# GpSimd takes over the softmax denominators, their reciprocals and v's step in a hybrid decoder layer

## The chip, the cores and the metric

The kernel runs on one core of a Trainium2 chip. The metric is the device time of one execution in microseconds. Three runs of the kernel before took 1414.54 to 1418.3 us, median 1416.7; one further execution was profiled. All times below are microseconds (us) unless marked ns.

## The reference

One layer over 4096 tokens of width 1024. x is normalised by its root mean square and projected by one matrix into nine column groups: pool input and gate (256 each), three conv groups (256 each), q (512), k and v (128 each) and the attention gate (512). Cut to the part that the change touches:

```python
def sliding_window_attention(q, k, v, sinks):      # 8 query heads of 64, 2 key/value heads, blocks of 128
    kb = concatenate([k of the block before, k of this block])
    vb = concatenate([v of the block before, v of this block])
    scores = einsum('bnqkgd,bnskd->bnkgqs', qb, kb)
    scores = where(valid, scores + alibi, -1e30)   # a query sees the 128 keys up to itself
    p = softmax(concatenate([scores, sink], -1), -1)[..., :-1]
    return einsum('bnkgqs,bnskd->bnqkgd', p, vb)
```

The result is multiplied by silu of its gate, joined with the pool and conv branches, multiplied by w_out and added to x, and the sum is normalised.

## The kernel before, in words

The work has three stages. **Attention** walks over the 4096 tokens in 8 blocks of 512 (`NB`), each of 4 subtiles of 128. The **mixer** makes the conv and pool branches, and the **output** stage multiplies by w_out, by a scheme that needs sums and differences of w_out's quarters; these 28 sums (`Combos`) are made during attention, five per block in blocks 1 to 5 and the rest in block 6, and parked in HBM. Every matrix product is made in three matmuls, from a high and a low part of each operand. Each engine has its own queue, written out by hand in order, and waits on semaphores that others raise.

A block of the attention stage, engine by engine:

- **TensorE** (`body`, L1332): the first attend of the block before (L1238, two subtiles of probabilities times v), four q projections (the last holds `fold_sums`, L271, the sums of squares of the next x), the second attend, the v projection, then scores of subtile 0, gate projection 0, scores 1, gate 1, scores 2, gate 2, scores 3, gate 3, and k of the next block. Scores of a subtile (L1293) wait until VectorE has taken those before, since they share one PSUM region (`wide`). v's four transposes (`turn_v`) stand inside scores 1. In the last block v stands behind scores 0. The second attend waits for the mean of the next x's squares (`rstd_steps`), and each attend for GpSimd's mask.
- **VectorE** (`body`, L1113): the low part of k, the output of the first attend times the gate (L1220), the transposition of the last subtile's probabilities (L1073), low parts of q (L1093), the sums of w_out (L488 add, L500 low part), half of the next x's squares (L248), the mean (L282), then for each half of the heads `take_scores` (L1031: fold both key tiles into one, add the bias, row maximum), its negation (L1053) and the sinks' difference (L1054), `invert` (L1061: denominator L1065, reciprocal L1068), the transposition of the probabilities one subtile later, v's step (L1155, the difference of neighbouring blocks of v), the gates (L1103) and the eight pieces of the next x's low part (L339).
- **ScalarE** (`body`, L912): high parts of k and q, high parts of the sums (L496), the other half of the squares (L239), the scaling of x (L294), v out of PSUM before and after its transposes (L885, L977), exps (L903; with the sinks' exp, L900), the gates' tanh (L910), the high parts of the next x (L333).
- **GpSimd** (`body`, L856): the masks of the two last subtiles of the block before (L854), the root for the next x (L288), and per subtile the eight scalings of probabilities (L844). The masks of subtiles 0 and 1 stand behind subtile 2's.
- **SP** (`sync`, L711) issues transfers in order: the next x's first half (ScalarE issues the other), probabilities to HBM and back (`store_probs`, `load_probs`, which rearrange them), the sums' stores, xT's two halves (L728), y. In the last block it loads the mixer's first three weight chunks, CB, CA and GP (1 MB each, half of it from ScalarE's queue), ahead of the last probabilities of block 6.

A mask tile multiplies the probabilities of half the keys; v's step is subtracted the other way round for the upper 64 partitions.

Of the kernel before, what the change touches and what calls it, by code (L numbers as in the profile page):

```python
# [569 lines left out]
def attention_programs(nc, ctx, w, combos, banks, region, xs, spare, x_first, x_first_loaded, xT, xT_stored, xT_scratch, y, y_stored, x, ln_g,  # L570
# [53 lines left out]
    inv = sb("inv", [P, 2, HEADS])  # L624

# [85 lines left out]
    def sync(sp):  # L711
# [54 lines left out]
        for c in (CHUNK_CB, CHUNK_CA, CHUNK_GP):  # L766
# [3 lines left out]
        load_probs(sp, NB - 2, 3)  # L770
        sp.wait_ge(xT_stored[PIECES - 1], 16)
# [16 lines left out]
    def gpsimd(pool):  # L788
# [31 lines left out]
        def make_seen():  # L820
# [3 lines left out]
            nc.gpsimd.memset(masks[:, 2 * P:3 * P], 1.0).then_inc(bias_step, 1)  # L824
            pool.wait_ge(bias_step, 10)
# [30 lines left out]
        def body(n):  # L856
# [18 lines left out]
    def scalar(act):  # L875
# [20 lines left out]
        def exps(n, j, kv):  # L896
# [3 lines left out]
            nc.scalar.activation(sinkexp[:, b, heads], sinkdiff[:, b, heads], ACT.Exp)  # L900
            for t in range(GROUP):
                h = kv * GROUP + t
                last = nc.scalar.activation(probs[b][:, h], probs[b][:, h], ACT.Exp,  # L903
                                            bias=negmax[:, b, h:h + 1], accum_out=rowsum[:, b, h:h + 1])
            last.then_inc(exp_done, 1)
# [6 lines left out]
        def body(n):  # L912
# [21 lines left out]
            if final:  # L934
                act.wait_ge(st.lo_done, KT * NB)
                for c in (CHUNK_CB, CHUNK_CA, CHUNK_GP):
                    w.load(act, c, (2, 3))
            q_hi(n, 0)
            for s in combos.of_block(n, (0,)):
                combos.split_hi(act, s)  # L940
            if first:
                w.split_hi(act, CHUNK_Q + 1)
            if not first and not final:
                act.wait_ge(free(slot("g3")), earlier(n - 1, slot("g3")) + 1)
                st.square(act, n + 1)
            q_hi(n, 1)
            for s in combos.of_block(n, (1,)):
                combos.split_hi(act, s)
            if first:
                w.split_hi(act, CHUNK_G)  # L950
                st.square(act, 1)
            q_hi(n, 2)
            for s in combos.of_block(n, (2,)):
                combos.split_hi(act, s)
# [5 lines left out]
            if not final:  # L960
                for part in (0, 1):
                    st.scale(act, n + 1, part)
            for s in combos.of_block(n, (3, 4)):
                combos.split_hi(act, s)
# [14 lines left out]
            if not final:  # L979
                take_v()  # L980
# [12 lines left out]
                exps(n, 2, 1)  # L993
                for kk in range(st.AHEAD):
# [3 lines left out]
                for kv in range(KV):  # L998
                    exps(n, 3, kv)
            else:  # L1000
                for kv in range(KV):
                    exps(n, 0, kv)
                take_v()
                for kv in range(KV):
                    exps(n, 1, kv)
                gate_tanh(n, 0)
                exps(n, 2, 0)
                spread_v()
                exps(n, 2, 1)
                gate_tanh(n, 1)  # L1010
                w.split_hi(act, CHUNK_GP)
                for kv in range(KV):
                    exps(n, 3, kv)
                for t in (2, 3):
# [5 lines left out]
    def vector(dve):  # L1020
# [10 lines left out]
        def take_scores(n, j, kv):  # L1031
# [15 lines left out]
            for h in range(kv * GROUP, (kv + 1) * GROUP):  # L1047
# [5 lines left out]
            nc.vector.tensor_scalar(negmax[:, b, heads], rowmax[:, b, heads], -1.0, None, ALU.mult)  # L1053
            nc.vector.tensor_tensor(sinkdiff[:, b, heads], sinks[:, heads], rowmax[:, b, heads],  # L1054
                                    ALU.subtract).then_inc(max_ready, 1)
# [4 lines left out]

        def invert(m, b, kv):  # L1061

            heads = slice(kv * GROUP, (kv + 1) * GROUP)
            dve.wait_ge(exp_done, 2 * m + kv + 1)
            nc.vector.tensor_tensor(denom[:, b, heads], rowsum[:, b, heads], sinkexp[:, b, heads],  # L1065
                                    ALU.add).then_inc(den_step, 1)
            dve.wait_ge(den_step, 4 * m + 2 * kv + 1)
            nc.vector.reciprocal(inv[:, b, heads], denom[:, b, heads]).then_inc(den_step, 1)  # L1068
# [44 lines left out]
        def body(n):  # L1113
# [8 lines left out]
            if not first:  # L1122
                output(dve, n - 1, 0)
                turn_squares_of_probs(SUB * n - 1)
            make_q_lo(n, 0)
            make_combos(n, (0,))
            if not first and not final:
                st.square_more(dve, n + 1)
            for t in range(1, GROUP):
                if first:  # L1130
# [4 lines left out]
                if t == 3 and not final:  # L1135
                    st.mean(dve, n + 1)
# [1366 lines left out]
```

## Time and profile before

| | |
|---|---|
| median of 3 runs | 1416.7 us (1414.54 to 1418.3) |
| the profiled execution | 1414.61 us, its span 1412.7 us |
| mean granted clock of TensorE | 0.991 |
| busy: TensorE, VectorE, ScalarE, GpSimd | 96%, 83%, 39%, 25% of the span |
| attention stage | from the start to about 634 us |

The profile is of one execution. An engine's busy time is the union of its instructions; idle time is put down to what released the engine. The granted clock is TensorE's, as a share of 2.4 GHz. A matmul's end is modelled, and matmuls overlap, so the busy share of TensorE doesn't tell its rate.

### The profile page before, as it was taken

The page shows a single profiled execution, that of the slowest core. Times are in us where ns is not written, and L with a number is a line of the kernel's source. Part 1 is how long each engine was busy: PE and PEld are TensorE (multiplying, and loading weights), DVE is VectorE, ACT ScalarE, POOL GpSimd, SP SyncE. Part 2 cuts the span into 40 slices and gives each one's busy share as a digit, 9 for nine tenths or more (in the row PEclk, how much of TensorE's full clock was granted, in tenths as well). Part 3 has the DMA queues.
Part 4 walks back from the last instruction along what each step waited for, and adds up shares of the span by engine and source line. Part 5 has one row for each costly group of instructions (what it writes and reads, how often), then busy time and mean ns, then how long its engine had stood idle before and what let it go on. Part 6 is the DMA issues. An engine that isn't in the chain of part 4 may idle for free.

```text
span 1412.7 us, 20609 instructions
## 1 busy us (share of the span) xinstructions
PE 1354.7 (96%) x7070; PEld 1114.6 (79%) x7070; DVE 1173.6 (83%) x2381; ACT 550.8 (39%) x1421; POOL 358.4 (25%) x543
## 2 busy tenths in 40 slices
PE   6998999999999999889999999999999999999998
PEld 5776877777778787768888888888888788888886
DVE  5786869596978776649899998988999998898886
ACT  5654646565646564412122112121132243333332
POOL 5131313232322231220101011010110355455552
PEclk9999999999999999999999999999999999999999
DMA  9658393958585756875213033031327575554531
GB/s 214 204 141 307 99 312 120 289 166 274 173 238 209 195 204 167 295 164 199 97 52 134 29 137 134 15 134 45 148 96 266 236 244 173 179 179 155 170 106 75
DMA packets 117547, 239.18 MB, mean 169 GB/s; under 512 B 17488, under 2 KB 75216, under 8 KB 109776
## 3 DMA queue, kind: packets, MB, share of 16 engines
q1 hardware_dynamic: 93312, 214.24, 45.6%
q10 hardware_dynamic: 24144, 23.80, 6.9%
q8 instruction: 49, 0.80, 0.2%
q14 instruction: 42, 0.34, 0.1%
HBM read 139.44 MB, written 98.57 MB: 168 GB/s over the span
## 4 chain that ended last, share of the span: by engine, by line
PE 60%; DVE 19%; DMA 10%; ACT 4%; issue 3%; SPq 2%; POOL 1%; POOLq 0%; DVEq 0%; ACTq 0%
PE wide L346 12%; PE wide L347 12%; PE wide L348 12%; DMA xs<-in_x_dram 4%; DVE a_rows L1048 3%; DVE xT L339 3%; DVE m_tail L2047 3%; PE pair L1271 2%; PE pair L1272 2%; PE pair L1277 2%; PE turn L346 2%; PE pair L346 2%; PE pair L348 2%; PE turn L348 2%; PE pair L347 2%
## 5 line engine op out<-in xcount | busy, mean ns | idle before, releaser
L2047 DVE SCALAR_TENSOR_TENSOR m_tail<-m_tail,m_taps 128x512 f32<-128x512 f32 x480 | 338.3, 749 | 4.6
L844 POOL TENSOR_SCALAR a_rows<-a_rows,a_inv 128x128 f32<-128x128 f32 x256 | 91.8, 378 | 266.1 <-DVE a_inv L1068 203.9
L1271 PE MATMUL pair<-xT,w_hi 128*128 128x512 f32 x384 | 151.8, 395 | 3.6 <-DVE w_lo L410 3.6
L1272 PE MATMUL pair<-xT,w_lo 128*128 128x512 f32 x384 | 150.6, 392 | 0.0
L1277 PE MATMUL pair<-xT,w_hi 128*128 128x512 f32 x384 | 148.6, 393 | 0.0
L1789 POOL TENSOR_TENSOR operand_sums<-m_y 128x512 f32<-128x512 f32 x75 | 101.9, 1359 | 167.8 <-PE wide L348 116.7
L346 PE MATMUL wide<-x_first,w_hi 128*128 128x512 f32 x320 | 125.4, 392 | 0.0
L346 PE MATMUL wide<-xT,w_hi 128*128 128x512 f32 x320 | 125.2, 391 | 0.0
L348 PE MATMUL wide<-x_first,w_hi 128*128 128x512 f32 x320 | 124.6, 389 | 0.0
L348 PE MATMUL wide<-xT,w_hi 128*128 128x512 f32 x320 | 124.6, 389 | 0.0
L347 PE MATMUL wide<-x_first,w_lo 128*128 128x512 f32 x320 | 124.5, 389 | 0.0
L347 PE MATMUL wide<-xT,w_lo 128*128 128x512 f32 x320 | 124.5, 389 | 0.0
L108 POOL TENSOR_TENSOR pool_carrier<-pool_carrier 128x1 f32<-128x1 f32 x23 | 14.1, 615 | 394.0 <-DVE m_meanvar L2056 394.0
L1876 ACT ACTIVATE x_first<-operand_sums 128x512 fp32r<-128x512 f32 x80 | 50.4, 632 | 153.8 <-POOL operand_sums L1789 152.5
L1271 PE MATMUL wide<-xT,w_hi 128*128 128x512 f32 x256 | 101.3, 396 | 0.0
L1272 PE MATMUL wide<-xT,w_lo 128*128 128x512 f32 x256 | 99.7, 390 | 0.0
L1277 PE MATMUL wide<-xT,w_hi 128*128 128x512 f32 x256 | 99.7, 390 | 0.0
L903 ACT ACTIVATE a_rows<-a_rows,a_negmax 128x128 f32<-128x128 f32 x256 | 98.7, 387 | 0.0
L1271 PEld LDWEIGHTS pair<-xT,w_hi 128*128 128x128 f32 x384 | 72.8, 190 | 18.9 <-DVE w_lo L410 4.0
L1277 PEld LDWEIGHTS pair<-xT,w_hi 128*128 128x128 f32 x384 | 72.5, 189 | 18.1 <-DVE xT L339 2.9
L1272 PEld LDWEIGHTS pair<-xT,w_lo 128*128 128x128 f32 x384 | 72.7, 189 | 13.7
L1048 DVE CUSTOM_DVE_ANT_0 a_rows<-wide,a_bias,a_sinks 128x128 f32<-128x128 f32 x256 | 74.6, 348 | 2.3
(264 smaller groups left out, 3107.6 us busy)
## 6 DMA issues: line engine op xcount, KB each, us to landing
xT_scratch<-xT SPq DMA_DIRECT2D x16, 2048.0 KB, 11.2
p_scratch<-a_rows SPq DMA_DIRECT2D x128, 128.0 KB, 2.4
x_first<-xT_scratch SPq DMA_DIRECT2D x16, 1024.0 KB, 8.8
xT<-xT_scratch SPq DMA_DIRECT2D x16, 1024.0 KB, 9.5
combo_scratch<-stage SPq DMA_DIRECT2D x28, 512.0 KB, 5.9
m_y<-y_scratch ACTq DMA_DIRECT2D x14, 1024.0 KB, 6.6
xs<-in_x_dram SPq DMA_DIRECT2D x20, 512.0 KB, 9.9
a_pT<-p_scratch SPq DMA_DIRECT2D x16, 512.0 KB, 3.6
```

What stands on the lines that cost most here:

```text
L346: nc.tensor.matmul(out, w_hi, x_hi, start=first, stop=False)
L347: nc.tensor.matmul(out, w_lo, x_hi, start=False, stop=False)
L348: return nc.tensor.matmul(out, w_hi, x_lo, start=False, stop=last)
L844: last = nc.gpsimd.tensor_scalar(probs[b][:, h], probs[b][:, h], inv[:, b, h:h + 1], 0.5, ALU.mult, ALU.mult)
L903: last = nc.scalar.activation(probs[b][:, h], probs[b][:, h], ACT.Exp, bias=negmax[:, b, h:h + 1], accum_out=rowsum[:, b, h:h + 1])
L1048: last = nc.vector.tensor_tensor_reduce(out=probs[b][:, h], in0=in_runs(score[:, h, P:]), in1=in_runs(bias[:, h]), scale=1.0, scalar=sinks ...
L1271: nc.tensor.matmul(out, w.hi(c)[:, kk, cols], st.hi[:, kk, :], start=(kk == 0), stop=False)
L1272: nc.tensor.matmul(out, w.lo(c)[:, kk, cols], st.hi[:, kk, :], start=False, stop=False)
L1277: last = nc.tensor.matmul(out, w.hi(c)[:, kk, cols], st.lo[:, kk, :], start=False, stop=(kk == KT - 1))
L1789: nc.gpsimd.tensor_tensor(operand_sums[:, i, 1], y_block(q, left), y_block(q, right), SIGN[op]).then_inc(operand_sum, 1)
L1876: nc.scalar.activation(operands[:, i, 0], operand_source(q, i), ACT.Copy).then_inc(operand_hi, 1)
L2047: nc.vector.scalar_tensor_tensor(out=conv[:, i, :], in0=h[:, i, j:j + TB], scalar=taps[:, i, j:j + 1], in1=conv[:, i, :], op0=ALU.mult, op ...
```

## The change

GpSimd forms the sinks' differences, the denominators, their reciprocals (a power with exponent -1 from a tile `minus_one`) and v's step in one instruction; the mask carries the sign for the upper half. VectorE loses these. ScalarE exponentiates the sinks after the probabilities of a half, and copies v behind subtile 1's second exps; v's transposes move from scores 1 to scores 2. The sums of w_out are made one place earlier among the parts of q, and their stores go ahead of xT's halves. VectorE takes both halves of scores 3 ahead of the splits of the next x. The last block loads GP later.

```diff
 # SP, blocks 1 to 6
                 load_probs(sp, n - 1, 2)
-                store_probs(sp, n - 1, 3)
                 for s in combos.of_block(n, (0,)):
                     combos.store(sp, s)
+                store_probs(sp, n - 1, 3)
                 load_probs(sp, n - 1, 3)
...
-            for s in combos.of_block(n, (1,)):
+            for s in combos.of_block(n, (1, 2)):
                 combos.store(sp, s)
             store_xT(n, 0)
-            for s in combos.of_block(n, (2,)):
+            for s in combos.of_block(n, (3, 4)):
                 combos.store(sp, s)
             store_xT(n, 1)
-            for s in combos.of_block(n, (3, 4)):
-                combos.store(sp, s)
...
-        for c in (CHUNK_CB, CHUNK_CA, CHUNK_GP):
+        for c in (CHUNK_CB, CHUNK_CA):
             w.load(sp, c, (0, 1))
         load_probs(sp, NB - 2, 2)
         store_probs(sp, NB - 2, 3)
         load_probs(sp, NB - 2, 3)
+        w.load(sp, CHUNK_GP, (0, 1))
 # GpSimd
+        def sink_difference(n, j):
+            m, b = SUB * n + j, j % 2
             for kv in range(KV):
-                pool.wait_ge(den_step, 4 * m + 2 * kv + 2)
+                heads = slice(kv * GROUP, (kv + 1) * GROUP)
+                pool.wait_ge(max_ready, 2 * m + kv + 1)
+                nc.gpsimd.tensor_tensor(sinkdiff[:, b, heads], sinks[:, heads], rowmax[:, b, heads],
+                                        ALU.subtract).then_inc(den_step, 1)
+        def step_of_v(n):
+            pool.wait_ge(v_ready, 2 * n + 1)
+            nc.gpsimd.tensor_tensor(v_step, v[:, 1:, :], v[:, 0:SUB, :], ALU.subtract).then_inc(v_ready, 1)
+        def normalise(n, j):
+            m, b = SUB * n + j, j % 2
+            for kv in range(KV):
+                heads = slice(kv * GROUP, (kv + 1) * GROUP)
+                pool.wait_ge(exp_done, 2 * m + kv + 1)
+                nc.gpsimd.tensor_tensor(denom[:, b, heads], rowsum[:, b, heads], sinkexp[:, b, heads],
+                                        ALU.add).then_inc(den_step, 1)
+                pool.wait_ge(den_step, 6 * m + 2 * kv + 3)
+                nc.gpsimd.tensor_tensor(inv[:, b, heads], denom[:, b, heads], minus_one[:], ALU.pow).then_inc(den_step, 1)
+                pool.wait_ge(den_step, 6 * m + 2 * kv + 4)
                 for t in range(GROUP):
...
-            for j in range(SUB):
+            for j in range(SUB - 1):
+                sink_difference(n, j)
                 normalise(n, j)
-                if j == 2:
-                    for i in (0, 1):
-                        mask(n, i)
+            step_of_v(n)
+            sink_difference(n, SUB - 1)
+            for j in (0, 1):
+                mask(n, j)
+            normalise(n, SUB - 1)
 # ScalarE, blocks 0 to 6, from the exps on
-                for kv in range(KV):
-                    exps(n, 0, kv)
+                exps(n, 0, 0)
+                sink_exp(n, 0, 0)
+                exps(n, 0, 1)
+                sink_exp(n, 0, 1)
                 act.wait_ge(st.squared_more, st.HALF * (n + 1))
                 gate_tanh(n, 0)
+                exps(n, 1, 0)
+                sink_exp(n, 1, 0)
                 st.scale(act, n + 1, 3)
-                exps(n, 1, 0)
+                exps(n, 1, 1)
+                sink_exp(n, 1, 1)
                 spread_v()
-                exps(n, 1, 1)
                 gate_tanh(n, 1)
                 exps(n, 2, 0)
+                sink_exp(n, 2, 0)
+                exps(n, 2, 1)
+                sink_exp(n, 2, 1)
                 gate_tanh(n, 2)
-                exps(n, 2, 1)
-                for kk in range(st.AHEAD):
+                for kk in (0, 1):
+                    st.split_hi(act, n + 1, kk)
+                exps(n, 3, 0)
+                for kk in range(2, st.AHEAD):
                     st.split_hi(act, n + 1, kk)
 # VectorE, blocks 0 to 6
-                step_of_v()
-                inverts(2)
                 gate_make(n, 2)
-                take_scores(n, 3, 0)
+                for kv in range(KV):
+                    take_scores(n, 3, kv)
                 for kk in range(KT):
                     st.split_lo(dve, n + 1, kk)
-                take_scores(n, 3, 1)
                 turn_squares_of_probs(SUB * n + 2)
                 gate_make(n, 3)
-                inverts(3)
 # TensorE, blocks 0 to 6
                 scores(n, 0)
                 project(n, "g0")
-                scores(n, 1, lambda: turn_v(n))
+                scores(n, 1)
                 project(n, "g1")
-                scores(n, 2)
+                scores(n, 2, lambda: turn_v(n))
```

## Rows read from the trace of the kernel before

**Rows 1.** The page's busy times (share of the span) and instructions of each engine.
```profile
PE 1354.7 (96%) x7070; PEld 1114.6 (79%) x7070; DVE 1173.6 (83%) x2381; ACT 550.8 (39%) x1421; POOL 358.4 (25%) x543
```

**Rows 2.** Table by stretch, blocks 1 and 5 of five: length, busy of each engine, PEclk, DMA, GB/s.
```profile
121.28:198.05 76.77, 71.07 (x439) 57.69 (x439) 58.73 (x168) 42.52 (x137) 19.64 (x37) 0.98 0.68 210
...
420.69:493.97 73.28, 70.91 (x438) 57.72 (x438) 58.25 (x167) 42.73 (x137) 19.72 (x37) 0.98 0.68 210
```

**Rows 3.** Waits of TensorE: line and releaser, us in total, times, longest.
```profile
PE turn L1238 <- POOL a_rows L854: 15.2, 3, 6.8
PE turn L1238 <- DVE a_meansq L282: 10.8, 5, 2.9
PE wide L1300 <- DVE a_rowmax L1048: 9.4, 9, 2.8
```

**Rows 4.** Table by stretch, TensorE alone: length, busy, PEclk, DMA, GB/s.
```profile
420.90:424.20 3.30, 3.30 (x34) 0.50 0.93 387
```

**Rows 5.** The chain that ended last, attends: start, us, what.
```profile
420.69 4.61 PE turn L1238 x64
...
493.97 3.00 PE turn L1238 x64
...
569.57 5.31 PE turn L1238 x64
```

**Rows 6.** Groups by line, ScalarE's exps and VectorE's small work: busy, mean ns, idle before.
```profile
L903 ACT ACTIVATE a_rows<-a_rows,a_negmax 128x128 f32<-128x128 f32 x256 | 98.7, 387 | 0.0
...
L1068 DVE RECIPROCAL a_inv<-a_denom 128x4 f32<-128x4 f32 x64 | 11.4, 178 | 2.2
...
L1155 DVE TENSOR_TENSOR a_pT<-a_v 64x512 f32<-64x512 f32 x16 | 10.9, 681 | 0.1
...
L1065 DVE TENSOR_TENSOR a_denom<-a_rowsum,a_sinkexp 128x4 f32<-128x4 f32 x64 | 10.2, 160 | 12.2 <-ACT a_rows L903 11.5
```

**Rows 7.** Timeline of GpSimd in the mixer, at 702 and at 1123 us: start, us.
```profile
702.44 0.71 POOL L1765 TENSOR_SCALAR m_var_eps<-m_meanvar 128x4 f32<-128x4 f32 x1
...
704.03 1.53 POOL L1768 TENSOR_TENSOR m_ln_rstd<-m_var_eps,neg_half 128x4 f32<-128x4 f32 x1
...
1123.25 0.20 POOL L1765 TENSOR_SCALAR m_var_eps<-m_meanvar 128x4 f32<-128x4 f32 x1 [7.18 <-DVE m_meanvar L2056]
...
1123.80 1.02 POOL L1768 TENSOR_TENSOR m_ln_rstd<-m_var_eps,neg_half 128x4 f32<-128x4 f32 x1
```

**Rows 8.** Timeline of GpSimd in block 5: four scalings, then a mask.
```profile
447.31 1.41 POOL L844 TENSOR_SCALAR a_rows<-a_rows,a_inv 128x128 f32<-128x128 f32 x4 [0.49 <-DVE a_inv L1068]
...
457.89 1.30 POOL L854 TENSOR_TENSOR a_pT<-a_pT,a_rows 128x512 f32<-128x512 f32 x1
```

**Rows 9.** Timeline of VectorE in block 5: subtile 1's transposition, and two negations of maxima.
```profile
450.02 1.24 DVE L1073 STREAM_TRANSPOSE a_rows<-a_rows 128x1024 f32<-128x1024 f32 x1
...
453.09 0.17 DVE L1053 TENSOR_SCALAR a_negmax<-a_rowmax 128x4 f32<-128x4 f32 x1
...
458.48 0.73 DVE L1053 TENSOR_SCALAR a_negmax<-a_rowmax 128x4 f32<-128x4 f32 x1
```

**Rows 10.** The chain that ended last, from 540 us: two neighbouring scores of the last block.
```profile
582.16 0.67 PE wide L1300 x8
589.44 0.67 PE wide L1300 x8
```

**Rows 11.** The chain that ended last: a sum's store, a load of x, a store of probabilities.
```profile
121.04 9.20 DMA combo_scratch<-stage
...
471.47 11.87 DMA xs<-in_x_dram
...
550.84 10.87 DMA p_scratch<-a_rows
```

More of the change, by code:

```diff
@@ L935, in body, with make_combos @@
                 act.wait_ge(st.lo_done, KT * NB)
-                for c in (CHUNK_CB, CHUNK_CA, CHUNK_GP):
+                for c in (CHUNK_CB, CHUNK_CA):
                     w.load(act, c, (2, 3))
+            def make_combos(slots):
+                for s in combos.of_block(n, slots):
+                    combos.split_hi(act, s)
+            make_combos((0,))
             q_hi(n, 0)
-            for s in combos.of_block(n, (0,)):
-                combos.split_hi(act, s)
             if first:
                 w.split_hi(act, CHUNK_Q + 1)
-            if not first and not final:
+            elif not final:
                 act.wait_ge(free(slot("g3")), earlier(n - 1, slot("g3")) + 1)
                 st.square(act, n + 1)
+            make_combos((1,))
             q_hi(n, 1)
-            for s in combos.of_block(n, (1,)):
-                combos.split_hi(act, s)
             if first:
@@ L951, in body @@
                 st.square(act, 1)
+            elif final:
+                w.load(act, CHUNK_GP, (2, 3))
+            make_combos((2,))
             q_hi(n, 2)
-            for s in combos.of_block(n, (2,)):
-                combos.split_hi(act, s)
+            make_combos((3,))
             if first:
@@ L959, in body @@
             q_hi(n, 3)
[L960 to L964, printed above, removed]
+            make_combos((4,))
             if final:
@@ L997, in body @@
                 st.split_hi(act, n + 1, KT - 1)
-                for kv in range(KV):
-                    exps(n, 3, kv)
+                sink_exp(n, 3, 0)
+                exps(n, 3, 1)
+                sink_exp(n, 3, 1)
             else:
@@ L1052, in take_scores @@
             dve.wait_ge(score_taken, 2 * m + kv + 1)
[L1053 to L1055 removed]
+            nc.vector.tensor_scalar(negmax[:, b, heads], rowmax[:, b, heads], -1.0, None,
+                                    ALU.mult).then_inc(max_ready, 1)
         def join_bias():
@@ L1123, in body @@
                 output(dve, n - 1, 0)
+            make_combos(n, (0,))
+            if not first:
                 turn_squares_of_probs(SUB * n - 1)
             make_q_lo(n, 0)
-            make_combos(n, (0,))
             if not first and not final:
@@ L1135, in body @@
                 if t == 3 and not final:
-                    st.mean(dve, n + 1)
+                    for s in combos.of_block(n, (4,)):
+                        combos.add(dve, s)
                 make_q_lo(n, t)
-                make_combos(n, (t,) if t < 3 else (3, 4))
                 if t == 2 and first:
                     join_bias()
+                if t == 2 and not final:
+                    st.mean(dve, n + 1)
                 if final and t >= 2:
                     w.split_lo(dve, CHUNK_CB + t - 2)
-            def inverts(j):
-                for kv in range(KV):
-                    invert(SUB * n + j, j % 2, kv)
+            for s in combos.of_block(n, (4,)):
+                combos.split_lo(dve, s)
             def next_x(part):
-                if not final:
-                    st.turn_squares(dve, n + 1, part)
-            def step_of_v():
-                dve.wait_ge(v_ready, 2 * n + 1)
-                for late, (to, of) in enumerate(((slice(1, 1 + SUB), slice(0, SUB)), (slice(0, SUB), slice(1, 1 + SUB)))):
-                    last = nc.vector.tensor_tensor(v_step[halves[late]], v[halves[late], to], v[halves[late], of], ALU.subtract)
-                last.then_inc(v_ready, 1)
+                st.turn_squares(dve, n + 1, part)
             if not first:
@@ L1162, in body @@
                     next_x(part)
-                for kv in range(KV):
-                    take_scores(n, 0, kv)
-                invert(SUB * n, 0, 0)
+            for kv in range(KV):
+                take_scores(n, 0, kv)
+            if not final:
                 next_x(2)
-                invert(SUB * n, 0, 1)
                 gate_make(n, 0)
@@ L1301, in by_k_lo, with by_k_hi @@
                                  start=(h % 2 == 0), stop=False)
+            def by_k_hi(h):
+                return nc.tensor.matmul(score[:, h, :], q[:, h, tokens], k_hi[:, h // GROUP, keys], start=False, stop=(h % 2 == 1))
             need(pe, score_taken, 2 * (m - 1) + 2)
@@ L1308, in scores @@
                 for h in range(kv * GROUP, (kv + 1) * GROUP):
-                    last = nc.tensor.matmul(score[:, h, :], q[:, h, tokens], k_hi[:, kv, keys],
-                                            start=False, stop=(h % 2 == 1))
+                    last = by_k_hi(h)
                 last.then_inc(score_full, 1)
```

43 lines of the change are left out of this document (22 added, 21 removed).

## The prediction

> **What bounds the kernel now.** I read the page's busy times first: TensorE is busy 96% of the span, no other engine above 83% [rows 1]. So a change can gain only TensorE's idle time, and what a lower clock costs. Next, the table by stretch, cut where TensorE starts a block's second attend (blocks 1 to 5; the first and the last of the five stand here): they take 76.77 to 73.28 us, 372.7 in all or 74.5 on average [rows 2]. TensorE's busy time in block 5 is 70.91.
>
> Then TensorE's waits [rows 3]: 15.2 us in three waits of an attend for GpSimd's mask (the longest, 6.8, opens the last attention block), 10.8 in five waits of the second attend for the mean of the next x's squares, 9.4 in nine waits of the scores for VectorE to have taken the scores before. After the longer waits comes a second loss. In the 3.3 us behind the wait at 420 us the granted clock is 0.50, the lower level of 1.2 GHz [rows 4]. The same 64 matmuls take 4.61 us there, 3.00 behind the shorter wait at 494 us, 5.31 at the start of the last block [rows 5]. So one such fall costs 1.61 us, and 2.31 in the last block. Of the 70.91 busy microseconds of block 5 it is 1.61: TensorE's own work in a block is 69.3.
>
> The chain of waits tells why the second attend is late. The load of the next x waits for the last piece of this x's split, takes 11.87 us to land, and its squares, the sums of w_out in between and the mean follow [rows 11]. In block 1 a stored sum took 9.20 us to land, queued behind half of xT, and the next sum waited for its buffer [rows 11].
>
> **The change, part by part.**
>
> *VectorE loses small work.* Per subtile and half, one add (160 ns), one reciprocal (178 ns) [rows 6] and the sinks' difference, of the add's size and so about 0.16; per block v's step, 2 x 681 ns [rows 6]. That is 8 x 0.50 + 1.36 = 5.4 us of a block's 58. VectorE isn't the bound, so this is worth only what its order delays: the takes of scores 3 now stand together ahead of the eight splits of x.
>
> *GpSimd gains it.* The kernel has operations of this shape (128x4) in the mixer, at two prices: 0.20 us, and 1.02 for a power, at 1123 us; 0.71 and 1.53 at 702 us, while VectorE runs its conv taps [rows 7]. These are the two bounds. The power here has exponent -1 where those have -0.5; nothing suggests another price. I take the low one: in the score stretch VectorE's large operations read PSUM on one side, unlike the taps, and the scalings between them run at 1.41 for four [rows 8], the mean of all 256. With 0.1 us between dependent steps a half then costs 0.30 + 0.30 + 1.12 + 1.41 = 3.1 us, a subtile 6.3, while scores come 7.28 us apart [rows 10]: GpSimd keeps pace, by 1 us. v's step is like a mask, 1.30 us [rows 8], and 8 x 1.7 + 1.3 = 15 us more on GpSimd's 20 per block is no bound by itself.
>
> Here stands a rule of the Trainium skill, "GPSIMD Engine Reference", § Engine selection: elementwise work costs about twice VectorE's time on GpSimd. By that estimate a half's three operations would cost 1.0 us in place of 1.4; the rows differ from it, since the power is 5.7 times the reciprocal.
>
> *The wait that this adds.* GpSimd now takes both halves' differences before the first denominator, so nothing is scaled until the second half's maximum is there. From that maximum to the last scaling: 0.3 + 2 x (0.3 + 1.1 + 1.41) = 5.9 us. Before: four exps of 0.39 [rows 6], 0.45 for add and reciprocal, 1.41, together 3.4. Probabilities come 2.5 us later. Before, subtile 1 was scaled at 447.31 + 1.41 = 448.7, and VectorE's transposition of it began at 450.02 [rows 8, 9]: slack 1.3. The transposition stands between the two takes of the next scores, which so slip by about 1 us. ScalarE adds one: the copy of v out of PSUM moves behind subtile 1's second exps and the sinks' exp (0.2), and delays the tanh, the gate and the next take. Together the fourth scores start 2.0 us late in each block; in block 5 they had no slack. Ends: 0 (GpSimd's latency is hidden by the takes saved) and 4 (both delays for two subtiles).
>
> *The splits of x.* Both takes of scores 3 come first, so TensorE's k projection waits for the last pieces: 0.7 us (0 to 1.1). A maximum's negation took 0.73 us once, in place of 0.17 as in its neighbours, when a mask had just begun on GpSimd [rows 8, 9]; more work there, so 0.6 a block.
>
> *Sums spread, stores ahead of xT.* SP now stores the third sum ahead of the first half of xT, and VectorE's sums stand ahead of ScalarE's copy of the same q part, so that each finds the other's work done. The 9.20 us landing and the scores' wait behind it go (2.8 us in block 1). But SP also stores the first sum ahead of the last probabilities of the block before; behind x (11.87 us for the last quarter [rows 11]) those are the queue's tail. So the mask, not the mean, is what ends last before the second attend; I give 1.1 us for what is left of that wait (0 to 3), short of the waits with a fallen clock.
>
> A block: 69.3 + 2.0 + 0.7 + 0.6 + 1.1 = 73.7 where it stays as it is, and 72.7 where the mask comes in time; I take the middle, 73.2, so 5 x 73.2 - 372.7 = **-6.7**.
>
> *Block 0* has no sums and no attend before it; it gets the scores' wait and loses part of its own: **+1.0** (-1 to +3).
>
> *The last block.* A third of the 3 MB of weights, GP, goes out behind the probabilities. Of those the last store, 0.5 MB behind the weights, took 10.87 us to land [rows 11]. At the 210 GB/s of the blocks [rows 2] 1 MB less in front of it is some 4.8 us. The split of x ends later by 1.5 (the 2.0 less what the earlier takes save), so the attend is released 3.3 us sooner, **-3.3**, and its wait no longer drops the clock, 5.31 - 3.00: **-2.3** [rows 5]. At the end of attention v's step and two masks now stand on GpSimd ahead of the last scalings, 3 x 1.3 = 3.9 us [rows 8]; what SP's queue hides of it no row tells (0 to 3.9), and I take **+2.8** at the last attend, which waits for the mask behind [rows 3]. GP's late arrival is covered by the block's second tanh, behind which its split stands.
>
> *Moved or added at no cost:* v's transposes behind the third scores (TensorE as long either way; the copy that waits for them is priced above), the memsets for -1 (once, at the start), the sign in the mask (same operation), the reordering of the q parts' hi and lo.
>
> **Sum:** -6.7 + 1.0 - 3.3 - 2.3 + 2.8 = -8.5 us. The profiled execution took 1414.6 (span 1412.7, 1.9 around it), 2.1 below the median of the runs, 1416.7. So 1406.1 in the profile's terms, **1408 us** as a median. Its own range, from the ends above, is 1402 to 1412.
>
> **Rivals.**
>
> *A. GpSimd becomes the bound: slower.* If its 128x4 operations cost what they cost beside the taps, a half is 0.81 + 0.81 + 1.63 + 1.41 = 4.7 us, a subtile 9.3, 2.0 more than the 7.28 between scores. It decides from 3.64 us a half, 0.5 above my price. The third and fourth scores then each wait 2 us more, 4 a block, 32 in eight: 1408 + 32 = 1440; half of the operations at that price, about 1424. For it: the row at 702, and the negation at 0.73. Against: the steady 1.41 of the scalings. Beside it stands a rule of the Trainium skill, "GPSIMD Engine Reference", § Key points: GpSimd shares its SBUF interfaces with VectorE and contends with instructions in a 2-port mode or with two SBUF inputs. The taps have two SBUF inputs, as the rule wants, and the rows at 702 agree with it. Chance 0.20.
>
> *B. The wait only moves: no change.* The fourth scores' 2.0 us is near the 2.9 at 420 us that came with a fallen clock. With 0.6 more the clock falls there: 1.6 x 7 = 11, 1419. Or the store of the first sum delays the last mask for its whole transfer: 75.2 a block, 5 x (75.2 - 73.2) = 10, 1418. Chance 0.25.
>
> *C. Waits gone altogether.* No late scores, the mask in time: 69.3 + 1.3 = 70.6 a block, 5 x 2.6 = 13 less, 1395. Against: GpSimd's latency, which no row can hide fully. Chance 0.07.
>
> That the change doesn't do what it says is true of one part: v's projection already stands ahead of the scores in blocks 0 to 6, so only its transposes move. That costs no chance.
>
> **How the numbers follow.** My forecast has 0.48. A measurement can tell about 0.3%, 4.2 us, from no change: below 1412.5 is faster, above 1421 slower. Faster is the forecast with C, 0.55; same is B, 0.25; slower is A, 0.20. The range, 1398 to 1427, takes in the forecast, B, and A up to half of its price; left out are most of C and A's upper part, under 0.2.
>
> **What would show it.** GpSimd's add near 0.2 and its power near 1.0 us; the wait of the second attend for the mean gone or under 1 us a block; a wait of about 2 us at the fourth scores in each block, on the row maximum, at full clock; the wait at the start of the last block under 4 us; blocks near 73. It is wrong if the 128x4 operations on GpSimd cost 0.7 and 1.5, if the scores' waits exceed 3 us, or if the second attend waits for the mask as long as it waited for the mean.

## The result, and the profile after

The changed kernel takes 1420.6 us (median of 20 runs, 1415.9 to 1423.6), the kernel before 1415.2 (median of 20): a ratio of 1.0029 over all runs, 95% interval 1.0019 to 1.0039 (the medians alone give 1.0038). It is **slower by 0.3%** where 1408 us, faster, was forecast; by the prediction's own bounds, up to 1421, that still counts as no change. The profiled spans differ by 6.8 us, 1419.5 against 1412.7, more than the 4.1 us of the ratio, so what follows accounts for this pair of executions.

The busy times of the page, to be read beside [rows 1]:

```profile
PE 1358.6 (96%) x7070; PEld 1111.6 (78%) x7070; DVE 1142.3 (80%) x2173; ACT 550.4 (39%) x1421; POOL 477.9 (34%) x745
```

The work has moved as meant: VectorE 31 us less, GpSimd 120 us more, still only a third of the span. TensorE gained nothing from it. The table by stretch, blocks 1 and 5 [rows 2], and then all five blocks as one stretch, before and after:

```profile
121.57:195.65 74.08, 70.15 (x438) 56.20 (x439) 54.69 (x141) 42.86 (x137) 34.34 (x62) 1.00 0.69 213
...
421.58:496.80 75.22, 71.78 (x438) 57.67 (x439) 54.55 (x141) 43.73 (x139) 34.41 (x63) 0.98 0.65 201
```

```profile
121.28:493.97 372.69, 353.44 (x2190) 287.19 (x2190) 292.28 (x834) 214.35 (x685) 98.63 (x185) 0.98 0.69 216
```

```profile
121.57:496.80 375.23, 354.09 (x2190) 283.84 (x2191) 273.21 (x704) 215.20 (x687) 172.84 (x311) 0.99 0.68 212
```

The five blocks are 2.5 us longer, 75.05 each, where 6.7 less was forecast. The rest is at the end of attention: from the second attend of block 6's queries, which stands in the last block, to the end of the last attend 69.33 us against 64.46, 4.9 more. Block 0 (+0.3) and block 6 (-0.8) make up the difference.

TensorE's waits, the columns of [rows 3]:

```profile
PE turn L1258 <- POOL a_rows L876: 19.2, 8, 7.7
PE wide L1320 <- DVE a_rowmax L1094: 12.3, 10, 1.8
...
PE pair L1297 <- DVE xT L339: 7.4, 21, 0.7
...
PE turn L1258 <- DVE a_meansq L282: 1.5, 1, 1.5
```

The wait for the mean is gone (10.8 to 1.5), as planned. In its place the attends wait for the mask in eight places where they did in three, and k's projection waits for the parts of x, a wait that TensorE did not have. Of the clock falls one was saved: five attends ran at 0.54 to 0.68 of the clock before, four run at 0.54 to 0.64 after. Four attends after, in the table by stretch (the clock stands third from the end): three at 0.54 to 0.62, and one undisturbed.

```profile
421.58:426.12 4.54, 4.54 (x64) 4.04 (x64) 3.41 (x5) 4.12 (x9) 2.72 (x1) 0.62 0.98 416
571.58:576.12 4.54, 4.54 (x64) 4.04 (x64) 2.29 (x1) 0.81 (x1) 0.00 (x0) 0.62 1.01 416
635.70:640.90 5.20, 5.20 (x64) 4.70 (x64) 0.00 (x0) 0.60 (x1) 0.30 (x3) 0.54 0.54 19
496.80:499.73 2.93, 2.93 (x64) 2.59 (x64) 1.00 (x2) 0.38 (x2) 2.73 (x1) 1.00 1.12 475
```

**GpSimd's prices came as assumed.** Its groups by line (busy, mean ns, idle before):

```profile
L866 POOL TENSOR_SCALAR a_rows<-a_rows,a_inv 128x128 f32<-128x128 f32 x256 | 96.0, 393 | 6.3
L862 POOL TENSOR_TENSOR a_inv<-a_denom,a_minus_one 128x4 f32<-128x4 f32 x64 | 67.7, 1059 | 5.0
...
L845 POOL TENSOR_TENSOR a_sinkdiff<-a_sinks,a_rowmax 128x4 f32<-128x4 f32 x64 | 18.2, 284 | 141.9 <-DVE a_negmax L1099 141.8
...
L859 POOL TENSOR_TENSOR a_denom<-a_rowsum,a_sinkexp 128x4 f32<-128x4 f32 x64 | 15.8, 247 | 0.0
```

A power is 1.06 us, an add 0.25, a difference 0.28. GpSimd sits idle for 142 us until the next maximum is there, so it has time to spare. That does not take its latency off the path: the next maximum waits, by way of VectorE's transposition, for GpSimd's scalings, as the last block shows below.

**The splits of x.** The stretch from the end of scores 3 to the end of k's projection in one block, first before, then after; the busy time is that of the eight splits (line 339) alone:

```profile
380.68:391.94 11.26, 6.42 (x8) 1.00 0.23 70
```

```profile
380.26:393.73 13.47, 7.47 (x8) 1.00 0.18 58
```

The same 48 projection matmuls of TensorE's take 2.2 us longer, and the splits one microsecond longer. What they meet is on GpSimd's timeline. Before:

```profile
383.73 1.30 POOL L854 TENSOR_TENSOR a_pT<-a_pT,a_rows 128x512 f32<-128x512 f32 x1
385.56 1.37 POOL L854 TENSOR_TENSOR a_rows<-a_rows 128x512 f32<-128x512 f32 x1 [0.53 <-DMA a_rows<-p_scratch]
```

VectorE's timeline at the first of these masks, before: a negation that takes 0.17 us elsewhere [rows 9].

```profile
383.78 1.26 DVE L1053 TENSOR_SCALAR a_negmax<-a_rowmax 128x4 f32<-128x4 f32 x1
```

After, GpSimd's two masks, and the splits that start in those 2 us (duration ns min/median/max):

```profile
386.53 1.81 POOL L876 TENSOR_TENSOR a_pT<-a_pT,a_rows 128x512 f32<-128x512 f32 x1
388.31 1.74 POOL L876 TENSOR_TENSOR a_rows<-a_rows 128x512 f32<-128x512 f32 x1
```

```profile
L339 DVE SCALAR_TENSOR_TENSOR xT<-xs,a_gain,xT x2: 1776/1784/1791, 387.1 to 388.8; 128x512 fp32r<-128x512 f32 x2
```

A split is 0.74 us, and 1.78 where a mask has just begun; a mask is 1.30, and 1.74 to 1.81 where a split has. In each of its first seven blocks the kernel before lost one split and one negation to its two masks. Afterwards both masks, which now stand behind the sinks' difference of subtile 3 and so behind the last maximum, fall on splits: 14 of 56 in place of 7. So the mean of a split goes from 868 to 1000 ns:

```profile
L339 DVE SCALAR_TENSOR_TENSOR xT<-xs,a_gain,xT 128x512 fp32r<-128x512 f32 x56 | 44.9, 868 | 0.0
```

```profile
L339 DVE SCALAR_TENSOR_TENSOR xT<-xs,a_gain,xT 128x512 fp32r<-128x512 f32 x56 | 52.2, 1000 | 0.0
```

**The second attend.** The chain that ended last, after, in one block: SP stores the first sum (404.31), then the last probabilities (406.03 and on), the last piece of which lands 7.72 us after its issue; load and mask follow, and TensorE.

```profile
404.31 0.59 SPq L506
...
406.03 0.40 SPq L696
...
407.46 7.72 DMA p_scratch<-a_rows
...
416.07 4.04 DMA a_rows<-p_scratch
...
420.17 1.27 POOL a_rows L876
421.44 0.14 issue
421.58 3.66 PE turn L1258 x33
```

### The profile page after: what moved, and what is told of

Its sections match the earlier page's. It is cut to its first block, busy times and chain, and to the rows that moved or that the text cites. A ratio compares the mean times of both kernels' runs of the same rounds, so it can differ in the third digit from the quotient of the medians.

```text
span 1419.5 us, 20603 instructions
## 1 busy us (share of the span) xinstructions
PE 1358.6 (96%) x7070; PEld 1111.6 (78%) x7070; DVE 1142.3 (80%) x2173; ACT 550.4 (39%) x1421; POOL 477.9 (34%) x745
## 4 chain that ended last, share of the span: by engine, by line
PE 56%; DVE 19%; DMA 10%; POOL 6%; issue 4%; ACT 3%; SPq 3%; POOLq 0%; DVEq 0%; ACTq 0%
PE wide L346 12%; PE wide L347 12%; PE wide L348 12%; DMA p_scratch<-a_rows 6%; DVE a_rows L1094 4%; DVE xT L339 4%; DVE m_tail L2069 3%; DVE wide L1090 3%; PE turn L1258 2%; POOL a_rows L866 2%; PE turn L346 2%; PE pair L346 2%; PE turn L347 2%; PE pair L347 2%; PE pair L348 2%
## 5 line engine op out<-in xcount | busy, mean ns | idle before, releaser
L1297 PE MATMUL pair<-xT,w_hi 128*128 128x512 f32 x384 | 154.3, 402 | 8.3 <-DVE xT L339 7.4
L1291 PE MATMUL pair<-xT,w_hi 128*128 128x512 f32 x384 | 152.0, 396 | 3.5 <-DVE w_lo L410 3.5
L108 POOL TENSOR_TENSOR pool_carrier<-pool_carrier 128x1 f32<-128x1 f32 x23 | 14.1, 613 | 395.0 <-DVE m_meanvar L2078 395.0
L866 POOL TENSOR_SCALAR a_rows<-a_rows,a_inv 128x128 f32<-128x128 f32 x256 | 96.0, 393 | 6.3
```

What stands on the lines that cost most here:

```text
L866: last = nc.gpsimd.tensor_scalar(probs[b][:, h], probs[b][:, h], inv[:, b, h:h + 1], 0.5, ALU.mult, ALU.mult)
L1291: nc.tensor.matmul(out, w.hi(c)[:, kk, cols], st.hi[:, kk, :], start=(kk == 0), stop=False)
L1297: last = nc.tensor.matmul(out, w.hi(c)[:, kk, cols], st.lo[:, kk, :], start=False, stop=(kk == KT - 1))
```

## The experiments

Each time stands as a ratio to the kernel before, measured on the same chip (95% interval); the changed kernel is 1.0029. Where k's stretch is given, it is that from scores 3 to k's end in block 4, 11.26 us before and 13.47 after. A difference to the changed kernel in us goes by the two ratios.

**1. The store of the last probabilities first.**
```
 load_probs(sp, n - 1, 2)
+store_probs(sp, n - 1, 3)
 for s in combos.of_block(n, (0,)): combos.store(sp, s)
-store_probs(sp, n - 1, 3)
```


> The changed kernel with one thing undone: SP stores the last probabilities of the block before ahead of the first sum, as the kernel before did. Order theory: the second attend waits for the mask only because that store goes out some 1.5 us later and behind three transfers; the wait (1.0 to 2.6 us a block) falls to the mean's, some 0.9, and its clock falls go: 6 x 0.9 + 3 x 1.6 = 10 us less, about 1410. Rival, the wait only moves: the mean, or the mask still, ends as late; the wait stays above 1.3 and the time within 3 us of 1420. Scores' wait 1.3 and k's wait 2.2 a block as in the changed kernel under both.

0.9981 (0.9971 to 0.9991), 1409.4 us: 0.5% less than the changed kernel, 7 us. The waits, and the five blocks, now at full clock throughout:

```profile
PE wide L1320 <- DVE a_rowmax L1094: 12.0, 9, 2.0
PE turn L1258 <- POOL a_rows L876: 11.2, 3, 7.8
...
PE pair L1297 <- DVE xT L339: 7.3, 21, 0.7
...
PE turn L1258 <- DVE a_meansq L282: 2.6, 2, 1.3
```

```profile
121.07:486.68 365.61, 350.73 (x2191) 281.01 (x2191) 273.06 (x702) 214.14 (x685) 173.53 (x310) 1.00 0.68 216
```

The mask waits are down from eight to three, and k's and the scores' waits are as they were. The order theory holds: one place in SP's queue costs the five blocks 9.6 us between these two profiles, and the whole 7 us by the ratios.

**2. The masks ahead of the sinks' difference.**
```
+for j in (0, 1): mask(n, j)
 step_of_v(n)
 sink_difference(n, SUB - 1)
-for j in (0, 1): mask(n, j)
 normalise(n, SUB - 1)
```


> The changed kernel with GpSimd's masks of subtiles 0 and 1 ahead of v's step and of the sinks' difference of subtile 3, for which it waits. Order theory: TensorE's k projection still waits 2.2 us a block, since both takes of scores 3 still stand ahead of the splits; only the last block gains, where the attend no longer waits for these masks (1.3) and the last scalings come some 2 us sooner: about 1417. Contention theory (the masks make the splits of x slow, and so k late): the masks meet the takes in place of the splits, k's wait falls to about 1.1 and the time to 1410.

1.0017 (1.0008 to 1.0026), 1.7 us less than the changed kernel; the intervals overlap a little. k's stretch stayed at 13.49: in this block the second mask and v's step met the splits in place of the two masks, and over all blocks 10 splits of 56 were still stretched. The contention theory's number missed, since the masks moved too little to clear the splits, and the run does not tell the theories apart.

**3. The second take of scores 3 behind the splits,** on top of 2.
```
-for kv in range(KV): take_scores(n, 3, kv)
+take_scores(n, 3, 0)
 for kk in range(KT): st.split_lo(dve, n + 1, kk)
+take_scores(n, 3, 1)
```


> As the run with the masks first, and VectorE takes the second half of scores 3 behind the eight splits of x, as the kernel before did. Order theory: the splits end 2.1 us sooner, k's wait of 2.2 falls under 0.3 in each of seven blocks, 14 us less: about 1404; the last probabilities come some 3 us later and their mask with them by at most 1 us, since the transposition stood behind the first sum anyway. Rival, the wait only moves: the mask for the second attend comes as much later as k is sooner, the attend waits 4 us a block, and the time stays near 1418.

1.0123 (1.0102 to 1.0144): much slower. k's stretch fell only to 12.90, as three splits of eight now met GpSimd's work, and the last probabilities came so much later that the attends waited for the mask 25.0 us in seven waits (14.7 in run 2).

The order theory's 1404 was wrong; the rival had it, as far as the wait moving goes. With GpSimd's part and the masks where they stand here, the new order of the takes is the better one.

**4. The two masks made small:** seven eighths of the two are left out.
```
+if not whole_mask: part, over_heads = part[:, :, 0:1, :], over_heads[:, :, 0:1, :]
 nc.gpsimd.tensor_tensor(part, part, over_heads, ALU.mult)
...
-    mask(n, j)
+    mask(n, j, False)
```


> The changed kernel with the masks of subtiles 0 and 1 applied to one of the eight heads only (seven eighths of those two masks are left out). If it is the masks that stretch single splits of x from 0.74 to 1.78 us (two in a block), no split takes over 1 us, they end 2.1 us sooner, and k's wait falls from 2.2 to about 0.2: 7 x 2 = 14 us less, 1406. If the stretched splits come from something else (the transfers, ScalarE), they stay at 1.78 and the time within 3 us of 1420.

0.9916 (0.9902 to 0.9930), 16 us less than the changed kernel. No split is over 0.82 us, and k's stretch is 11.52:

```profile
L339 DVE SCALAR_TENSOR_TENSOR xT<-xs,a_gain,xT 128x512 fp32r<-128x512 f32 x56 | 38.6, 757 | 0.0
```

It is the masks that stretch the splits. The 16 us are not the splits' alone: subtile 3's scalings stand behind these masks on GpSimd and come sooner too, and the run does not divide the two.

**5. GpSimd's part undone** in the changed kernel (differences, adds, reciprocals, v's step on VectorE).
```
-nc.gpsimd.tensor_tensor(denom[:, b, heads], rowsum[:, b, heads], sinkexp[:, b, heads], ALU.add)
-nc.gpsimd.tensor_tensor(inv[:, b, heads], denom[:, b, heads], minus_one[:], ALU.pow)
...
+nc.vector.tensor_tensor(denom[:, b, heads], rowsum[:, b, heads], sinkexp[:, b, heads], ALU.add)
+nc.vector.reciprocal(inv[:, b, heads], denom[:, b, heads])
...
+for j in range(SUB):
+    normalise(n, j)
+    if j == 2:
+        for i in (0, 1): mask(n, i)
...
```


> The changed kernel with GpSimd's part undone: differences, adds, reciprocals and v's step on VectorE where the kernel before has them, masks behind the scalings of subtile 2; all other orders as changed. If the part is nearly neutral (VectorE idled there, GpSimd keeps pace), the time stays within 3 us of the changed kernel's 1.003 of before, and k's wait falls only by the one mask that then meets the takes and not the splits (2.2 to about 1.2). If GpSimd's latency is what made the kernel slower, the scores' wait falls from 1.3 to under 0.5, all probabilities come 2.5 us sooner and the time falls to 0.995 of before.

0.9954 (0.9939 to 0.9969), 10.7 us less than the changed kernel. That is the time of the second theory, but not by its mechanism: the scores' wait stays (12.3 us in 8 waits; 12.3 in 10 in the changed kernel), while k's stretch is 12.27 and the mean of a split 762 ns. One mask per block falls on a negation, none on a split of blocks 1 to 6.

**6. Masks of subtiles 0 and 1 on VectorE,** with 1.
```
 take_scores(n, 2, 1)
+mask_early(n, 0)
...
 for kk in range(KT): st.split_lo(dve, n + 1, kk)
+mask_early(n, 1)
...
-for j in (0, 1): mask(n, j)            # on GpSimd
...
+nc.vector.tensor_tensor(part, part, over_heads, ALU.mult).then_inc(masked, 1)
```


> The run with the store first (0.998 of before), and the masks of subtiles 0 and 1 made on VectorE: the first in its idle time ahead of the third gate product, the second behind the splits. Contention theory: no split over 0.9 us, k's wait 2.2 to about 0.4 in seven blocks, 13 us less: 0.989 of before. Rival: the two masks cost VectorE 0.7 each on the same path and the second delays the first attend by as much; k's wait falls, the first attend waits 1 us, and some 5 us are left: 0.995.

0.9863 (0.9839 to 0.9886): better than both theories' numbers. A mask is 0.68 us here, and every split takes its 0.74:

```profile
L1116 DVE TENSOR_TENSOR a_pT<-a_pT,a_rows 128x512 f32<-128x512 f32 x8 | 5.5, 684 | 0.0
```

```profile
L339 DVE SCALAR_TENSOR_TENSOR xT<-xs,a_gain,xT 128x512 fp32r<-128x512 f32 x56 | 37.8, 740 | 0.0
```

```profile
120.01:478.09 358.08, 347.44 (x2192) 281.90 (x2191) 271.28 (x713) 214.34 (x685) 155.59 (x301) 1.00 0.71 222
```

k's stretch is 11.97. The 0.7 us over that of before hold the order of the takes, the first mask, which now stands ahead of them on VectorE, and 0.2 us in which the attend behind k waits for the second mask; no run tells these apart. Nor was it tried to give VectorE the masks and the small work both.

**7. Two chains ahead of the fourth scores shortened,** with 1: each half's sink difference directly ahead of its own denominators, and the second tanh ahead of the copy of v.
```
 heads = slice(kv * GROUP, (kv + 1) * GROUP)
+sink_difference(n, j, kv)
 pool.wait_ge(exp_done, 2 * m + kv + 1)
...
+act.wait_ge(v_turned, n + 1)
+gate_tanh(n, 1)
 spread_v()
-gate_tanh(n, 1)
```


> The run with the store first (0.998 of before), with two waits ahead of the fourth scores shortened: GpSimd forms a half's difference directly ahead of that half's denominators, so that it does not wait for the second half's maximum, and ScalarE makes the second tanh ahead of the copy of v. If these two chains set the fourth scores' wait (1.3), it falls to about 0.4 and the splits start as much sooner: 7 x 0.9 = 6 us less, 0.994. If what is gained there is only waited again by k for the splits, k's wait grows from 2.2 to 3.1 and the time stays at 0.998.

0.9965 (0.9950 to 0.9980), which overlaps with run 1: inconclusive in time. The scores' waits fell from 12.0 to 7.9 us, and the second attends wait for the mean again (7.8 us in five waits). The edit did a third thing: the masks no longer stand behind subtile 3's second maximum, and no split is stretched. They fall on two negations a block, so the stall moved and did not go:

```profile
381.24 1.12 DVE L1098 TENSOR_SCALAR a_negmax<-a_rowmax 128x4 f32<-128x4 f32 x1
384.19 0.66 DVE L1098 TENSOR_SCALAR a_negmax<-a_rowmax 128x4 f32<-128x4 f32 x1
```

The splits of block 4 take 5.40 us as in run 6, k's wait falls from 7.3 to 1.1 us in all, and yet k's stretch is 12.82. So clean splits alone do not bring that stretch back to 11.26, nor the time down.

**8. All of it together,** and v's step, the third gate product and the last load moved too.
```
-gate_make(n, 2)
 for kv in range(KV): take_scores(n, 3, kv)
+gate_make(n, 2)
...
+if j == 2 and n < NB - 1: step_of_v(n)
 normalise(n, j)
```


> All of it: store first, masks of subtiles 0 and 1 on VectorE, halves in turn, second tanh ahead of the copy of v, and also v's step on GpSimd ahead of subtile 2, the third gate product behind both takes of scores 3, and at the end of attention the load of the last probabilities ahead of the 1 MB of weights U. If the three waits (k 2.2, scores 1.3, second attend) are separate costs, a block falls to about 70.5, the last attend comes some 5 us sooner, and the time is 0.98 of before, about 1385. If one engine's chain takes up what the others lose, it is no better than 0.989.

0.9892 (0.9867 to 0.9917): no better than run 6. k's wait is gone (11.03), but the scores wait 14.1 us in 15 places (13.6 in run 6), and the second attends wait 6.7 us for the mean (2.3 in run 6). The rival's number was right: what one wait loses another takes up.

**9. Run 6, and the last probabilities loaded ahead of U's weights.**
```
+attention.turn_loads(sp)
 w.load(sp, CHUNK_U)
-attention.turn_loads(sp)
```


> The run with the masks on VectorE (0.986 of before), and at the end of attention SP loads the last probabilities ahead of the 1 MB of weights U, as in the run with all together, where the stretch to the last attend was 5 us shorter. If that is a gain, the last attend no longer waits 7 us and the time is 0.983 of before. Rival: U's weights come as much later and the mixer's first projections wait for them; 0.986.

**0.9844 (0.9830 to 0.9859), 1392.0 us: the fastest, ahead of both kernels;** its interval overlaps with run 6's. All waits for GpSimd's masks together, the last attend's among them, are 2.9 us where the changed kernel has 19.2; VectorE's masks add 1.4:

```profile
PE turn L1268 <- POOL a_rows L876: 2.9, 2, 1.6
```

**10. GpSimd's part alone, in the kernel before.**
```
+for j in range(SUB - 1):
+    sink_difference(n, j)
+    normalise(n, j)
+for j in (0, 1): mask(n, j)
+step_of_v(n)
+sink_difference(n, SUB - 1)
+normalise(n, SUB - 1)
...
-invert(SUB * n, 0, 0)
...
-inverts(3)
```


> The kernel before with GpSimd's part alone (differences, adds, powers, v's step), the two masks right behind subtile 2 and every other order as before. If GpSimd's later probabilities and the masks beside the splits are the cost of the change, two or three splits a block take 1.78 us in place of one, the scores wait longer, and the time is 1.005 to 1.010 of before. If GpSimd's part is neutral by itself, 0.998 to 1.002.

1.0084 (1.0056 to 1.0112). 15 of 56 splits are stretched, and the scores wait 19.7 us in 14 places where before it was 9.4 in nine [rows 3]:

```profile
L339 DVE SCALAR_TENSOR_TENSOR xT<-xs,a_gain,xT 128x512 fp32r<-128x512 f32 x56 | 55.9, 1064 | 0.8 <-ACT xT L333 0.7
```

The part that gives the change its name makes the kernel slower by itself. It adds 0.8% to the kernel before, and as much to the kernel of run 5, which is the changed kernel without it (0.9954 to 1.0029), though the masks stand in another place in the two. So the part costs some 11 us either way, and the other edits win back part of it.

**11. All but GpSimd's part, with the store first:** the edits of run 5 and
```
+store_probs(sp, n - 1, 3)
 for s in combos.of_block(n, (0,)): combos.store(sp, s)
-store_probs(sp, n - 1, 3)
```


> The changed kernel without GpSimd's part (0.995 of before) and with the store of the last probabilities ahead of the first sum: what is left is the new order of VectorE, ScalarE, TensorE and the sums. If the store's place costs the second attend its waits here too, they fall to under 1 us a block, the lower clock goes, and the time is 0.990. If the mean then ends as late, 0.995.

0.9905 (0.9890 to 0.9919). The new orders together are worth about 13 us, once the store stands where it did; they were not tried one by one. The store's place is worth 0.5% here too (0.9954 to 0.9905), as in run 1.

**12. GP's weights back ahead of the last probabilities.**
```
-for c in (CHUNK_CB, CHUNK_CA): w.load(sp, c, (0, 1))
+for c in (CHUNK_CB, CHUNK_CA, CHUNK_GP): w.load(sp, c, (0, 1))
...
-w.load(sp, CHUNK_GP, (0, 1))
...
```


> The changed kernel with GP's 1 MB of weights loaded where the kernel before loads it, ahead of the last probabilities of the block before the last. If those probabilities are then late, as forecast, the attend that opens the last block waits 6 to 7 us in place of 2.4 and the time is 4 us longer, 1.006 of before. If the transfer's place does not set that wait, it stays at 1.003.

1.0041 (1.0028 to 1.0054), against 1.0029 (1.0019 to 1.0039): 1.7 us more, within the intervals. In the profile TensorE's gap ahead of that attend is 4.3 us in place of 2.4, so in that gap the transfer is worth 1.9 of the 3.3 forecast.

## Why the prediction was wrong

Of the 15.3 us between the forecast's -8.5 and the profile's +6.8, the five blocks make 9.2 and the blocks behind them 6.9; block 0 came 0.7 better than forecast. Two steps failed in the blocks, the second attend and the splits of x, and a third at the end.

**GpSimd's prices (right) and its pace (right but for the last block).** The low price held, and rival A, which had GpSimd as the bound at 0.71 and 1.53, did not come to pass. But its sign was right: GpSimd's part costs some 11 us (runs 5 and 10). The reason is one that the forecast had in hand and applied to the wrong instructions: the stalls between the two engines.

**The splits of x: the term that was mis-sized.** "0.7 us (0 to 1.1)" became 2.2. The masks, which wait for the sinks' difference and so run beside the splits, are 1.95 of it (run 4: 13.47 to 11.52, all orders as changed). What the order costs by itself stays open: with clean splits k's stretch is 11.97, 12.27 and 12.82 in runs 6, 5 and 7, whose other edits also move it. The step "A maximum's negation took 0.73 us once ... so 0.6 a block" saw the cause, but only for the negations. It also misread how often: the trace before has one such negation in each of seven blocks, of 0.72 to 1.26 us. These got cheaper: none of them takes over 0.33 us after. It never asked where the two masks would land, although the mean of a split before, 868 ns for an operation of 740, said that one in eight was already paying.

Here the Trainium skill has the rule, "SBUF — State Buffer", § SBUF: two separate sides: VectorE and GpSimd have one pair of SBUF ports in common, taken as an exclusive lock for a whole instruction by whichever starts first, where VectorE's operation has two SBUF inputs or runs in a two-port mode. The trace agrees for the masks: the first (386.53) runs 0.5 us over its 1.30, the split that starts at 387.1 in turn 1.04 over its 0.74, and it ends only after the mask does. Of GpSimd's 128x4 operations it shows one side alone: they take longer beside the splits (0.64 and 1.41 us, last section), and no split does beside them.

**The second attend: the step that failed.** "So the mask, not the mean, is what ends last before the second attend; I give 1.1 us for what is left of that wait (0 to 3), short of the waits with a fallen clock." The order of events was right and the amount was not. SP issues the first sum and two loads of w_out for 1.7 us (404.31 to 406.03) ahead of the store, whose last piece then takes 7.72 us to land (7.30 in run 1). TensorE's gaps ahead of the second attends are 0.2 to 2.6 us, and the clock fell behind the three over 2.3. At the end of the five blocks the gaps average 1.8 us and two falls add 0.6 a block: 2.4, where the sum had 0.5, the middle of a wait of 1.1 and none. Run 1 has 0.5 and no fall there, and is 7 us faster. Rival B's second form had this delay at 2.0 a block, nearly exact; that its sum comes out too (75.2 us a block, 1418; measured 75.05 and 1420.6) needs the cancelling told below.

**The scores' wait** was forecast at 2.0 a block and is 1.3. Run 7, which shortens both of the chains named for it at once, takes a third off the waits (12.0 to 7.9 us); which of the two chains does it was not tried.

**The sum.** With the store put back the five blocks average 73.1 us, the forecast 73.2. That is luck in part: k's 1.5 too little stands against 0.7 too much for the scores and 0.6 for the negations. So the store's place is what the blocks' sum missed on balance.

**The last block.** Forecast -3.3, -2.3 and +2.8; measured +4.1 with block 6. The wait at its start did fall (6.8 to 2.4), but the attend still ran at 0.62 of the clock and took 4.54 us. Behind it the chain shows what was under-priced:

```profile
588.71 0.68 DVE wide L1090
...
597.79 0.68 DVE wide L1090
...
606.88 0.68 DVE wide L1090
...
609.04 2.17 POOL a_sinkdiff L845
611.21 1.25 POOL a_pT L876
612.46 1.24 POOL a_rows L876
613.83 3.05 PE turn L1258 x64
...
622.84 11.41 issue
634.29 1.27 POOL a_rows L876
635.70 5.28 PE turn L1258 x64
```

Line 1090 opens a take of the second half of a subtile's scores. These takes come 9.1 us apart, where scores came 7.28 apart before [rows 10]: between two of them the chain runs through GpSimd's denominators, powers and scalings and the transposition behind them. The forecast held GpSimd's 6.3 us a subtile against 7.28; the loop also holds the transposition and the take. Then a difference of 128x4 takes 2.17 us, while VectorE splits GP's weights (2.29 us). The masks wait for it and hold up first the attend at 613.83 and then the last scalings. The last load lands behind U's weights, as before, and the last attend runs at 0.54 of the clock (5.2 us; 4.2 before). Run 9 puts that load ahead of U's weights.

Run 7, in which the masks do not wait for subtile 3's second maximum nor a half's scalings for the other half's, needs 65.8 us for the stretch of 69.3. But run 5, without GpSimd's part, needs 69.4 too: there VectorE waits 3.4 us for a store of probabilities to land, and the scores behind it as long. So the 4.9 us cannot be put down to GpSimd alone, and what the later load of GP costs there stays open.

## What to carry to other kernels

Work moved from VectorE to GpSimd is not free because GpSimd has time: ask which wide operations with two SBUF operands will then run at the same moment on both engines. Here the narrow operations (128x4) on GpSimd stretched no split of VectorE's and the wide masks did, and of the splits of work tried the best was the reverse for those: masks on VectorE at 0.68 us, small work on GpSimd (run 6, 0.9863, against 0.9905 in run 11). An engine's idle time does not show that its latency is harmless: ask whether what it waits for waits for it. When a store is the head of a chain that ends at the busiest engine, look at its place in the queue: one place cost 7 us here.

## What the runs showed of the hardware

- A mask on GpSimd costs VectorE 1.04 us in one stalled split (1.78 for 0.74), more than the 0.68 us that VectorE needs to make the mask itself.
- The stall also hits a 128x4 negation with one SBUF input (1.26 for 0.17 us), and GpSimd's small operations beside the splits: 0.64 and 1.41 us for an add and a power that are 0.20 and 1.02 elsewhere:

```profile
390.00 0.64 POOL L859 TENSOR_TENSOR a_denom<-a_rowsum,a_sinkexp 128x4 f32<-128x4 f32 x1
390.72 1.41 POOL L862 TENSOR_TENSOR a_inv<-a_denom,a_minus_one 128x4 f32<-128x4 f32 x1
```
- Rival A's two prices of [rows 7] would fit one price without and with such a stall: both operations cost 0.51 us more while VectorE runs its taps. No run here varies that.
